# Half-size tiles for the score levels, and a new order at the stage edges, in a two-layer HGRN2/GLA encoder step

## The chip, the cores and the metric

The kernel runs on one core of a Trainium2 chip. The metric is the device time of one execution in microseconds (us). Engines are named as in the profile: PE is the matrix engine's matmuls, PEld its weight loads (they overlap the matmuls), DVE the vector engine, ACT the scalar engine, POOL the GpSimd engine, SP the engine whose queue issues the DMAs.

## The reference

Two groups of tokens go through the same two layers: 1024 tokens of one prompt, and 8 streams of 16 tokens each. Together they are 1152 tokens, nine tiles of 128.

```
layer 0: m = hgrn2_mixer(x)   # 8 heads, key width 128, value width 128
layer 1: m = gla_mixer(x)     # 4 heads, key width 128, value width 256
x = layer_norm(ALPHA * x + m);  x = layer_norm(ALPHA * x + conv_ffn(x))   # in both layers

# both mixers, per head, logf the log of a data-dependent forget gate:
b      = cumsum(logf)
scores = einsum('td,sd,tsd->ts', q, k, exp(b[t] - b[s]))      # s <= t
o      = scores @ v + (q * exp(b)) @ S
S_new  = exp(b_last) * S + (k * exp(b_last - b)).T @ v
```

The feed-forward part is `gelu(causal_conv3(a)) * b @ w_down` with `[a|b] = x @ w_up` and 2816 columns.

## The kernel before

**Matmuls.** Each weight and each activation is split into a rounded part (`_hi`) and a remainder (`_lo`), and a product is three matmuls (`mm3`, L770 to L772). Products that aren't split are plain float32 matmuls; the trace shows two PE instructions for each of those (x16 for eight tiles).

**Scores by levels.** Within a tile of 128 tokens the scores are found in seven levels, `LEVELS = [64, 32, 16, 8, 4, 2, 1]`. At level m a query in the second half of a block of 2m tokens meets the keys in the first half of that block, both decayed to the block's middle. For level x the DVE subtracts (`sub`, L1579), ACT takes the exponentials, the DVE multiplies by k and q (`decay`, L1595 and L1596), PE multiplies per token tile (L1021), and the DVE copies what the level's mask allows from PSUM to the score tile `a` (`place_scores`, L1608). A matmul of level x loads `128 - m` keys (at least 68) as weights and streams 64 queries. The first three levels of prompt tiles have 8 tiles (the streams' blocks begin at m = 8), the others 9. The last level is a matmul of 128 keys by 192 columns per tile (L1005), whose diagonal and pair scores are copied by L1621 and L1629. The prompt's scores go to banks 0 and 1 by turns, those of the last level to banks 1 to 5.

**A head.** PE's order in a head is written out: the projection of the next head's keys or queries, the transposes of the decayed keys (L891), the streams' part (L899, eight matmuls by turns on four groups of 32 output partitions), states (L912, L933), the second projection, outputs (L965, L967), and then the list `MERGED`: level 0, value/gate tiles 0 and 1, then level x followed by value/gate tile x + 1. A value/gate tile is 24 matmuls. In the h layer, `rest_early` (L1647) makes the remainders of the next head's weights on the DVE, in levels 4 and 5 of the list.

**Waits that the change touches.** `scores_taken` makes the next head's first projection wait until all scores are out of PSUM, since it writes banks 0 to 2. The last transposes of a layer wait for the same and for the last value tile. At the edge between the layers POOL splits the first GLA head's value and gate weights, and their DMAs wait until the rank-16 projection (`r_pe`) is done. `AFTER` lists which transposes follow which sum of the output projection; a normalized tile `("n", t)` must be ready on the DVE (L1519) before it is transposed. `last_outputs` is the DVE's order at the end of a layer's mixer, `gate` (L1804, L1806) within it.

## Time and profile before

| | |
|---|---|
| median of 3 runs | 2972.05 us (2970.08 to 2974.06) |
| the profiled execution's own time | 2972.53 us |
| its span, first to last instruction | 2970.7 us |
| granted clock, mean | 0.993 |
| PE busy | 2915.5 us, 98% |
| DVE, ACT, POOL busy | 1654.6, 711.7, 913.0 us |

PE is busy nearly all the time, so the table of busy shares alone says little; what matters is how long each PE instruction holds the engine, and the few places where PE stands idle. The granted clock is TensorE's, as a share of 2.4 GHz.

### The profile page before, as it was taken

Reading aid. Unit: us, or ns where it says so; the run is one execution under the profiler, and the core shown is the slowest. Engines: PE = TensorE matmul, PEld = TensorE weight load, DVE = VectorE, ACT = ScalarE, POOL = GpSimd, SP = SyncE. Lnnn points to the kernel's source line nnn. Section 1 sums busy time; section 2 is a strip of 40 time slices with the busy share of each in tenths; the row PEclk is TensorE's granted clock in tenths of the full one; section 3 lists DMA queues with packets and bytes.
Section 4 is the critical chain, followed back from the end, with each engine's and each line's share of the span. In section 5 each row is a group of like instructions: output and inputs, shape, how many; then the busy total and the mean of one; then the engine's idle time right before and its main releaser. Section 6 shows DMA issues by size and latency. Waiting matters only on the chain.

```text
span 2970.7 us, 41990 instructions
## 1 busy us (share of the span) xinstructions
PE 2915.5 (98%) x16893; PEld 2706.4 (91%) x16893; DVE 1654.6 (56%) x2229; ACT 711.7 (24%) x1332; POOL 913.0 (31%) x396
## 2 busy tenths in 40 slices
PE   8999999999999999999998999999999999999998
PEld 8999999978999999999987888887899999999997
DVE  5777777776544444444465456557654444444446
ACT  4444444431111111111123334332111111111112
POOL 2111111131533333333236214213153333333324
PEclk9999999999999999999999999999999999999999
DMA  4111111131111111111022112204111111111102
GB/s 127 44 44 43 43 43 43 57 111 36 57 43 43 42 42 42 42 42 42 29 77 92 40 35 72 65 22 123 39 57 43 43 42 41 42 41 41 42 30 92
DMA packets 189918, 155.82 MB, mean 52 GB/s; under 512 B 7144, under 2 KB 173120, under 8 KB 189760
## 3 DMA queue, kind: packets, MB, share of 16 engines
q1 hardware_dynamic: 189836, 154.64, 16.8%
q8 instruction: 61, 1.00, 0.1%
q14 instruction: 21, 0.17, 0.0%
HBM read 135.34 MB, written 19.28 MB: 52 GB/s over the span
## 4 chain that ended last, share of the span: by engine, by line
PE 91%; DVE 4%; ACT 2%; issue 1%; POOL 1%; DMA 0%; POOLq 0%; SPq 0%; ACTq 0%; DVEq 0%
PE psum L770 27%; PE psum L772 27%; PE psum L771 27%; PE psum L1021 4%; PE psum L1005 1%; PE psum L804 1%; PE psum L912 1%; DVE stats L1505 1%; ACT h_junk L1197 0%; PE psum L965 0%; PE psum L891 0%; POOL ring_lo L703 0%; PE psum L967 0%; DVE tm L1955 0%; PE psum L933 0%
## 5 line engine op out<-in xcount | busy, mean ns | idle before, releaser
L700 POOL TENSOR_TENSOR ring_hi<-ring_raw,ones 128x1024 fp32r<-128x1024 f32 x181 | 388.8, 2148 | 1930.5 <-DMA ring_raw<-in_ffn_w_up 724.1
L770 PE MATMUL psum<-xt_hi,ring_hi 128*128 128x384 f32 (+1 forms) x2712 | 914.0, 337 | 13.3 <-DVE h_a L1629 4.3
L771 PE MATMUL psum<-xt_lo,ring_hi 128*128 128x384 f32 (+1 forms) x2712 | 911.5, 336 | 0.0
L772 PE MATMUL psum<-xt_hi,ring_lo 128*128 128x384 f32 (+1 forms) x2712 | 911.3, 336 | 0.0
L770 PEld LDWEIGHTS psum<-xt_hi,ring_hi 128*128 128x128 f32 (+1 forms) x2712 | 510.2, 188 | 25.8 <-issue 6.6
L771 PEld LDWEIGHTS psum<-xt_lo,ring_hi 128*128 128x128 f32 (+1 forms) x2712 | 510.3, 188 | 3.0 <-issue 0.4
L772 PEld LDWEIGHTS psum<-xt_hi,ring_lo 128*128 128x128 f32 (+1 forms) x2712 | 510.3, 188 | 2.2 <-issue 0.5
L703 POOL TENSOR_TENSOR ring_lo<-ring_raw,ring_hi 128x1024 fp32r<-128x1024 f32 x181 | 461.7, 2551 | 14.2
L770 PE MATMUL psum<-ring_hi,xt_hi 128*128 128x256 f32 (+1 forms) x1152 | 399.7, 347 | 4.9 <-POOL ring_lo L703 4.9
L772 PE MATMUL psum<-ring_hi,xt_lo 128*128 128x256 f32 (+1 forms) x1152 | 388.9, 338 | 0.0
L771 PE MATMUL psum<-ring_lo,xt_hi 128*128 128x256 f32 (+1 forms) x1152 | 388.4, 337 | 0.0
L1919 DVE TENSOR_TENSOR tm<-tm,psum 128x512 f32<-128x512 f32 x360 | 247.5, 688 | 242.4 <-PE psum L772 237.2
L770 PE MATMUL psum<-ring_hi,h_hi 128*128 128x512 f32 x792 | 309.1, 390 | 0.0
L772 PE MATMUL psum<-ring_hi,h_lo 128*128 128x512 f32 x792 | 308.8, 390 | 0.0
L771 PE MATMUL psum<-ring_lo,h_hi 128*128 128x512 f32 x792 | 308.7, 390 | 0.0
L1888 DVE TENSOR_SCALAR cv<-ax,params 128x1024 f32<-128x1024 f32 x88 | 52.8, 643 | 435.2 <-ACT ax L1197 435.2
L1197 ACT ACTIVATE ax<-psum 128x384 f32<-128x384 f32 (+2 forms) x176 | 67.5, 411 | 853.5 <-PE psum L772 853.5
L770 PEld LDWEIGHTS psum<-ring_hi,xt_hi 128*128 128x128 f32 x1152 | 219.4, 190 | 26.6 <-POOL ring_lo L703 5.3
L772 PEld LDWEIGHTS psum<-ring_hi,xt_lo 128*128 128x128 f32 x1152 | 219.0, 190 | 23.4
L771 PEld LDWEIGHTS psum<-ring_lo,xt_hi 128*128 128x128 f32 x1152 | 219.5, 191 | 21.0
L1890 DVE SCALAR_TENSOR_TENSOR cv<-ax,params,cv 128x1024 f32<-128x1024 f32 (+1 forms) x176 | 213.1, 1252 | 10.4 <-DVE cv L1888 3.2
L772 PEld LDWEIGHTS psum<-ring_hi,h_lo 128*128 128x128 f32 x792 | 148.7, 188 | 30.9
(198 smaller groups left out, 2978.2 us busy)
## 6 DMA issues: line engine op xcount, KB each, us to landing
ring_raw<-in_ffn_w_up SPq DMA_DIRECT2D x88, 512.0 KB, 3.8
ring_raw<-in_ffn_w_down SPq DMA_DIRECT2D x44, 512.0 KB, 3.9
tm<-in_x_prompt SPq DMA_DIRECT2D x16, 512.0 KB, 6.7
ring_raw<-in_hgrn_w_in SPq DMA_DIRECT2D x16, 512.0 KB, 5.3
ring_raw<-in_hgrn_w_in SPq DMA_DIRECT2D x32, 256.0 KB, 3.7
ring_raw<-in_gla_w_in SPq DMA_DIRECT2D x32, 256.0 KB, 4.1
x_scratch<-tm SPq DMA_DIRECT2D x9, 512.0 KB, 2.6
tm<-x_scratch SPq DMA_DIRECT2D x9, 512.0 KB, 6.9
```

Of the source, the lines that this page charges most:

```text
L700: nc.gpsimd.tensor_tensor(ring_hi[slot][:, 0:width], ring_raw[slot][:, 0:width], ones[:, :].to_broadcast([P, width]), ALU.mult).then_inc(u ...
L703: nc.gpsimd.tensor_tensor(ring_lo[slot][:, 0:width], ring_raw[slot][:, 0:width], ring_hi[slot][:, 0:width].bitcast(F32), ALU.subtract).the ...
L770: nc.tensor.matmul(dst, w_hi, x_hi, start=start, stop=False)
L771: nc.tensor.matmul(dst, w_hi, x_lo, start=False, stop=False)
L772: return nc.tensor.matmul(dst, w_lo, x_hi, start=False, stop=stop)
L804: last = nc.tensor.transpose(w_bank(layer, job)[:, k * P:(k + 1) * P], tm[:, t, kk * P:(kk + 1) * P], ident[:, :])
L912: last = nc.tensor.matmul(bank[b][:, x * dv:(x + 1) * dv], tile["kt"][:, c, :], tile["v"][:, c, :], start=True, stop=True)
L1021: last = nc.tensor.matmul(scores(x, t).rearrange("p (g w) -> p g w", w=m), ct[:, 0:level_keys(x)], queries, start=True, stop=True)
L1197: return nc.scalar.activation(*a, **k)
L1888: ins = V.tensor_scalar(dst, tap(0), param(f, 0), param(f, 3), ALU.mult, ALU.add)
L1890: ins = V.scalar_tensor_tensor(dst, tap(j), param(f, j), dst, ALU.mult, ALU.add)
L1919: V.tensor_tensor(x, x, bank[6 + n][:, :], ALU.add).then_inc(AD.sem, 1)
```

## The change

All levels under 64 tokens, and the last one, are made in two halves of a token tile: 64 keys as weights, half of the queries (32, or 96 columns in the last level) streamed, and the result written to output partitions 0 to 63 or 64 to 127. A block of at most 64 tokens lies wholly in one half, so the scores that are left out are those that the mask threw away. Matmul instructions double, columns per instruction halve. The DVE copies by halves too. The last level's scores go to banks 3 to 5.

Beside this: `rest_early` moves behind `place_scores(NL - 2)`; the next head's first projection no longer waits for the last level's copies; a layer's last transposes use banks 0 to 2 and wait neither for the copies nor for the last value tile; the GLA gate's low-rank matmuls of chunks 1 and 2 move behind the streams' states; the DMAs of three of the first GLA head's four value/gate units are issued ahead of the last two stores of x2, and POOL splits them in the order 0, 2, 3, 1; the last two token tiles of layer 1's input are transposed within the projection of chunk 1; tile n0 is transposed after sum 5 and n1 after sum 6 of the output projection; the feed-forward's first b chunk goes ahead of the last a chunk; the last DVE work of a mixer is reordered; POOL's third output unit waits for `gated`; in the very first head ACT takes the key exponential ahead of a value tile. A remainder is the `_lo` part of a split.

```diff
-AFTER[4], AFTER[5] = [("n", 0)], [("n", 1)]
+AFTER[5], AFTER[6] = [("n", 0)], [("n", 1)]
 for _t in range(EARLY, NT):
     if _t + 2 < NT:
-        AFTER[2 * _t] = [("o", _t + 2)]
+        AFTER[2 * _t] = AFTER[2 * _t] + [("o", _t + 2)]
...
+        def key_banks(last_):
+            return ((0, 0, 4), (1, 4, 8), (2, 8, 9)) if last_ else ((6, 0, 4), (3, 4, 8), (4, 8, 9))
...
+        def in_halves(x):
+            return LEVELS[x] < HALF
+        def half_scores(x, t, hf):
+            c = 0 if t == PT else t * (HALF // 2)
+            return level_bank(x, t == PT)[hf * HALF:(hf + 1) * HALF, c:c + HALF // 2]
...
-        def pair_scores(t):
-            c = t % 2 * 2 * P
-            return bank[1 + t // 2][:, c:c + 3 * HALF]
+        def pair_scores(t, hf):
+            return psum[hf * HALF:(hf + 1) * HALF, 3 + t // 4, t % 4 * P:t % 4 * P + 3 * HALF // 2]
...
+                    for u in GLA_FIRST_UNITS[:-1]:
+                        vg_unit(KIND["g"], 0, u)
                 sp.wait_ge(ln_done, NT + t + 1)
                 sp.dma_start(x2_dram[t * P:(t + 1) * P, :], tm[:, t, :]).then_inc(res_io[t], 16)
+            sp.wait_ge(SIG["g"]["r_pe"].sem, 3)
+            vg_unit(KIND["g"], 0, GLA_FIRST_UNITS[-1])
...
+                    if u == 2:
+                        pool.wait_ge(S["gated"].sem, S["gated"].at(heads, 0))
...
+            for x, u in enumerate(GLA_FIRST_UNITS):
+                split(U_G + 2 + x, 2 + u, slot_count("g", 0, 2 + u), skipped=4)
...
-                        wait("pred", i - 1, preds_after(LAST - 1) if c == 0 else S["pred"].per)
+                        wait("pred", i - 1, preds_after(LAST - 1))
...
-                    wait("vg", p, NT)
-                    if last_:
-                        wait("pred", p, S["pred"].per)
-                    for jb, (b, tiles) in enumerate(((6, range(0, 4)), (3, range(4, 8)), (4, range(8, 9)))):
-                        for x, t in enumerate(tiles):
+                    for jb, (b, t0, t1) in enumerate(key_banks(last_)):
+                        if b == 3:
+                            wait("pred", p, S["pred"].per)
+                        if b == 6:
+                            wait("vg", p, NT)
+                        for x, t in enumerate(range(t0, t1)):
                             last = nc.tensor.transpose(bank[b][:, x * P:(x + 1) * P], tile["c0"][:, t * P:(t + 1) * P], ident[:, :])
                         last.then_inc(S["kt_pe"].sem, 1)
+                    wait("vg", p, NT)
...
+                def low_rank(chunks):
                     pe.wait_ge(S["wgk_in"].sem, S["wgk_in"].at(i, 16))
                     pe.wait_ge(S["rt"].sem, 3)
-                    for c in range(NC):
+                    for c in chunks:
...
+                if n == "g" and not last_:
+                    low_rank(range(0, 1))
...
+                    low_rank(range(1, NC))
...
-                                last = nc.tensor.matmul(pair_scores(t), tile["k"][:, t * P:(t + 1) * P],
-                                                        tile["q3"][:, t * HALF:(t + 1) * HALF, :].rearrange("p g w -> p (g w)"),
-                                                        start=True, stop=True)
+                                for hf in range(2):
+                                    q0 = t * HALF + hf * (HALF // 2)
+                                    last = nc.tensor.matmul(pair_scores(t, hf), tile["k"][:, 2 * q0:2 * q0 + HALF],
+                                                            tile["q3"][:, q0:q0 + HALF // 2, :].rearrange("p g w -> p (g w)"),
+                                                            start=True, stop=True)
...
+                                if in_halves(x):
+                                    for hf in range(2):
+                                        ch = c[:, t * P + hf * HALF:t * P + (hf + 1) * HALF]
+                                        queries = ch.rearrange("p (g w) -> p g w", w=2 * m)[:, :, m:2 * m]
+                                        last = nc.tensor.matmul(half_scores(x, t, hf).rearrange("p (g w) -> p g w", w=m), ch, queries,
+                                                                start=True, stop=True)
+                                    continue
...
+                    weights_split(0)
+                    pe.wait_ge(F["a_out"].sem, F["a_out"].at(0, 0))
+                    for c in range(NC - 1):
+                        pe.wait_ge(tj_lo, w_job(layer, "n", TPC * (c + 1) - 1, 1) + 1)
+                        chunk(0, c)
+                    pe.wait_ge(ln_done, (2 * layer + 1) * NT)
+                    for hf in range(2):
+                        transpose_half(layer, "n", NT - 1, hf)
+                    weights_split(1)
+                    pe.wait_ge(params_rd, layer + 1)
+                    pe.wait_ge(F["mult"].sem, F["mult"].at(0, 0))
+                    chunk(1, 0)
+                    pe.wait_ge(tj_lo, w_job(layer, "n", NT - 1, 1) + 1)
+                    chunk(0, NC - 1)
+                    for c in range(1, NC):
+                        chunk(1, c)
...
+                            if c == 1 and (done, k) in (("q_proj", 0), ("q_proj", 6)):
+                                next_operand(NT - 2 if k == 0 else NT - 1)
...
+                if not ahead:
+                    take_vg(NL - 1)
                 wait("kh_sub", i, 2)
                 activate(tile["c0"][:, :], tile["c0"][:, :], ACT.Exp, scale=-K["scale"]).then_inc(S["kh_exp"].sem, 1)
+                if ahead:
+                    take_vg(NL - 1 + ahead)
...
+                            if in_halves(x):
+                                w = HALF // 2
+                                for hf in range(2):
+                                    h = slice(hf * HALF, (hf + 1) * HALF)
+                                    dst = tile["a"][h, t0:t1, h].rearrange("p t (g w) -> p t g w", w=2 * m)[:, :, :, m:2 * m]
+                                    src = level_bank(x, t0 == PT)[h, 0:nt * w].rearrange("p (t g w) -> p t g w", t=nt, w=m)
+                                    msk = level_mask[h, x * HALF + hf * w:x * HALF + (hf + 1) * w].rearrange("p (g w) -> p g w", w=m)
+                                    last = V.copy_predicated(dst, msk.unsqueeze(1).to_broadcast([HALF, nt, w // m, m]), src)
+                                last.then_inc(S["pred"].sem, 1)
+                                continue
...
-                    if n == "h" and x in (4, 5):
-                        rest_early(x - 4)
...
+                if n == "h":
+                    rest_early(0)
+                    rest_early(1)
...
                 chain_states(K, p, True)
+                gate(K, p)
                 new_streams(K, p, True, range(STREAMS_FIRST[n]))
-                for t in range(1, EARLY):
-                    rest_half(layer, "o", t, 0)
-                gate(K, p)
...
-                    take_o(K, p, True, (0, 1))
+                    take_o(K, p, True, (0,))
+                    rest_half(layer, "o", 1, 0)
+                    take_o(K, p, True, (1,))
                     apply_gate_early()
                     take_o(K, p, True, (2,))
                     apply_rms_early()
+                    rest_half(layer, "o", 2, 0)
                     take_o(K, p, True, (3,))
```

On PE, in the first h head, this is the end of the level list; `h_c` is the decayed key/query tile, `ring` the value/gate weights. Before, PE's rows read:

```order
L771 MATMUL psum<-ring_lo_79,xt_hi 128x256
L772 MATMUL psum<-ring_hi_78,xt_lo 128x256
L1021 MATMUL psum<-h_c_106 126x64 x9
L1005 MATMUL psum<-h_q_113,h_k 128x192 x9
L770 MATMUL psum<-ring_hi_75,xt_hi 128x256
L771 MATMUL psum<-ring_lo_76,xt_hi 128x256
L772 MATMUL psum<-ring_hi_75,xt_lo 128x256
```

In the change, PE's rows at the same place read:

```order
L801 MATMUL psum<-ring_lo_79,xt_hi 128x256
L802 MATMUL psum<-ring_hi_78,xt_lo 128x256
L1062 MATMUL psum<-h_c_106 64x32 x18
L1044 MATMUL psum<-h_q_113,h_k 64x96 x18
L800 MATMUL psum<-ring_hi_75,xt_hi 128x256
L801 MATMUL psum<-ring_lo_76,xt_hi 128x256
L802 MATMUL psum<-ring_hi_75,xt_lo 128x256
```

Both levels have twice the matmuls, with 64 weight columns and half of the streamed ones; nothing else has moved between the value/gate matmuls.

On the DVE, in the same head, from the subtraction of level 3 on; `h_a` is the score tile, `h_b` the running sum of log gates, and `ring_lo` the remainders. Before, the DVE's rows read:

```order
L1579 TENSOR_TENSOR h_c_105<-h_b 128x1152
L1608 COPY_PREDICATED h_a<-level_mask,psum 112x32x16
L1647 TENSOR_TENSOR ring_lo_70<-ring_raw_71,ring_hi_69 128x1024
L1595 TENSOR_TENSOR h_c_105<-h_c_105,h_k 128x144x4
L1596 TENSOR_TENSOR h_c_105<-h_c_105,h_q 128x144x4
L1579 TENSOR_TENSOR h_c_106<-h_b 128x1152
L1608 COPY_PREDICATED h_a<-level_mask,psum 120x64x8
L1608 COPY_PREDICATED h_a<-level_mask,psum 120x8x8
L1647 TENSOR_TENSOR ring_lo_73<-ring_raw_74,ring_hi_72 128x1024
L1595 TENSOR_TENSOR h_c_106<-h_c_106,h_k 128x288x2
L1596 TENSOR_TENSOR h_c_106<-h_c_106,h_q 128x288x2
```

In the change, the DVE's rows read so, from the last level's copy of level 4's scores on:

```order
L1677 COPY_PREDICATED h_a<-level_mask,psum 64x8x8x4 x2
L1677 COPY_PREDICATED h_a<-level_mask,psum 64x8x4 x2
L1657 TENSOR_TENSOR h_q_113<-h_q_113,h_q 128x576
L1735 TENSOR_TENSOR h_c_105<-h_b 128x128
L1738 TENSOR_TENSOR h_c_105<-h_b 128x1024
L1743 COPY h_dec<-h_e 128x8
L1744 COPY h_dec<-h_e 128x8
L1677 COPY_PREDICATED h_a<-level_mask,psum 64x8x16x2 x2
L1677 COPY_PREDICATED h_a<-level_mask,psum 64x16x2 x2
L1724 TENSOR_TENSOR ring_lo_70<-ring_raw_71,ring_hi_69 128x1024
L1724 TENSOR_TENSOR ring_lo_73<-ring_raw_74,ring_hi_72 128x1024
L1755 TENSOR_TENSOR h_c_105<-h_c_105,h_k 128x1152
```

The two `ring_lo` rows stood between the levels' copies and multiplications; they now stand behind the copies of level 5 and ahead of the multiplication (128x1152) that the key transposes wait for.

On SP's queue, at the edge between the layers (`x_scratch` is the stored x2, `ring_raw_77`, `80`, `83` and `86` are the four slots of value/gate units). Before, SP's rows read:

```order
L670 DMA x_scratch<-tm 128x1024 x7
L667 DMA ring_raw_74<-in_gla_w_in 128x8x128
L670 DMA x_scratch<-tm 128x1024 x2
L517 DMA ring_raw_77<-in_gla_w_in 128x2x256 x2
L517 DMA ring_raw_80<-in_gla_w_in 128x2x256 x2
L517 DMA ring_raw_83<-in_gla_w_in 128x2x256 x2
L517 DMA ring_raw_86<-in_gla_w_in 128x2x256 x2
L526 DMA g_s_142<-in_state_gla 128x8x256
```

In the change, SP's rows there read:

```order
L694 DMA x_scratch<-tm 128x1024 x7
L689 DMA ring_raw_74<-in_gla_w_in 128x8x128
L549 DMA ring_raw_77<-in_gla_w_in 128x2x256 x2
L549 DMA ring_raw_83<-in_gla_w_in 128x2x256 x2
L549 DMA ring_raw_86<-in_gla_w_in 128x2x256 x2
L694 DMA x_scratch<-tm 128x1024 x2
L549 DMA ring_raw_80<-in_gla_w_in 128x2x256 x2
L539 DMA g_s_142<-in_state_gla 128x8x256
```

Three of the four units are now issued ahead of the last two stores; the fourth, whose slot holds the rank-16 weights, stays behind them.

## Rows read from the trace of the kernel before

**Rows 1.** The page, busy time of each engine

```profile
PE 2915.5 (98%) x16893; PEld 2706.4 (91%) x16893; DVE 1654.6 (56%) x2229; ACT 711.7 (24%) x1332; POOL 913.0 (31%) x396
```

**Rows 2.** Waits of PE: total us, times, longest

```profile
PE psum L804 <- DVE tm L1519: 5.2, 3, 2.8
PE psum L770 <- POOL ring_lo L703: 4.9, 1, 4.9
PE psum L770 <- DVE h_a L1629: 4.3, 1, 4.3
...
PE psum L770 <- DVE g_s L1737: 3.2, 3, 1.1
PE psum L770 <- DVE xt_lo L1499: 3.1, 2, 1.6
PE psum L804 <- DVE tm L1768: 2.4, 1, 2.4
...
PE psum L891 <- DVE h_a L1629: 0.9, 1, 0.9
PE psum L891 <- issue: 0.8, 1, 0.8
```

**Rows 3.** Timeline of PE, levels 1, 5 and 6 of h head 2

```profile
205.71 1.57 PE L1021 MATMUL psum<-h_c 128*96 128x64 f32 x16 [0.42 <-DVE h_c L1596]
207.09 0.36 PE L770 MATMUL psum<-ring_hi,xt_hi 128*128 128x256 f32 x1
...
224.09 2.09 PE L1021 MATMUL psum<-h_c 128*126 128x64 f32 x18
225.98 0.37 PE L770 MATMUL psum<-ring_hi,xt_hi 128*128 128x256 f32 x1
...
228.93 3.09 PE L1005 MATMUL psum<-h_q,h_k 128*128 128x192 f32 x18
231.73 0.42 PE L770 MATMUL psum<-ring_hi,xt_hi 128*128 128x256 f32 x1
```

**Rows 4.** Groups of PE by form, level 0

```profile
L1021 PE MATMUL psum<-h_c 128*68 128x64 f32 x128 | 9.2, 225 | 1.1 <-DVE h_c L1596 1.1
```

**Rows 5.** Timeline of PE, the streams' part of h head 1

```profile
178.71 0.65 PE L899 MATMUL psum<-h_s,h_qz 128*32 128x128 f32 x16
179.35 0.38 PE L912 MATMUL psum<-h_v,h_kt 128*128 128x128 f32 x1
```

**Rows 6.** Window of 0.05 us, L899 alone: us, PE busy (in flight), PEld busy (in flight)

```profile
178.70:178.75 0.05, 0.04 (x4) 0.05 (x7) 1.00 0.00 0
```

**Rows 7.** Timeline of PE: first of 24 matmuls with 16, then 128 weight columns

```profile
1571.36 0.34 PE L770 MATMUL psum<-xt_hi,ring_hi 128*16 128x384 f32 x1
...
1575.52 0.34 PE L770 MATMUL psum<-xt_hi,ring_hi 128*128 128x384 f32 x1
```

**Rows 8.** Timeline of the DVE, levels 2 to 4 of h head 2

```profile
209.22 1.35 DVE L1579 TENSOR_TENSOR h_c<-h_b 128x1152 f32<-128x1152 f32 x1
...
211.90 0.76 DVE L1595 TENSOR_TENSOR h_c<-h_c,h_k 128x576 f32<-128x576 f32 x1 [0.68 <-ACT h_c L1197]
...
213.24 1.35 DVE L1579 TENSOR_TENSOR h_c<-h_b 128x1152 f32<-128x1152 f32 x1
...
215.11 1.22 DVE L1647 TENSOR_TENSOR ring_lo<-ring_raw,ring_hi 128x1024 fp32r<-128x1024 f32 x1
```

**Rows 9.** Window at head 1's first projection: PE, PEld, DVE, ACT, POOL busy, clock

```profile
92.00:99.00 7.00, 4.92 (x15) 4.92 (x16) 6.96 (x7) 0.00 (x0) 6.92 (x3) 0.51 0.01 2
```

**Rows 10.** Timeline of POOL at the edge between the layers

```profile
1593.97 1.89 POOL L700 TENSOR_TENSOR ring_hi<-ring_raw,ones 128x1024 fp32r<-128x1024 f32 x1 [8.89 <-DMA ring_raw<-in_gla_w_in]
```

**Rows 11.** Timeline of PE, two waits of layer 1 and what follows the first

```profile
1615.53 0.80 PE L770 MATMUL psum<-ring_hi,xt_hi 128*128 128x512 f32 x1 [4.95 <-POOL ring_lo L703]
...
1629.28 2.50 PE L1021 MATMUL psum<-g_c 128*68 128x64 f32 x32
...
2013.60 1.01 PE L965 MATMUL psum<-g_v,g_a 128*128 128x256 f32 x2 [1.99 <-DVE g_v L1793]
```

108 lines of the change are left out of this document (56 added, 52 removed).

## The prediction

> **What bounds the kernel now.** I read the page's busy times first: PE is busy 2915.5 us, and its weight loads 2706.4 [rows 1]. So the time is what PE's instructions take one after another, plus a few waits. The waits of PE came next. Those of over 1 us are few, and each has one cause [rows 2]. Then I read the timeline of a steady h head. There the distance from one row's start to the next group's start is what the group costs, since matmuls overlap: level 1 costs 207.09 - 205.71 = 1.38 us for 16 instructions, level 5 costs 1.89 for 18, the last level 2.80 for 18 [rows 3]. Levels 2, 3 and 4 read the same way: 1.50, 1.81 and 1.86. The six levels that change cost 11.24 us in a head, and twelve heads have them: 135 us.
>
> What holds such an instruction? Level 5 streams 64 columns and takes 1.89 / 18 = 105 ns. Level 0 streams 64 too, but loads 68 weight columns instead of 126, and takes (9.2 / 8 - 0.225) / 15 = 62 ns [rows 4]. So levels 1 to 5 are bound by the load of weights, at some 0.83 ns a column (105 / 126). The last level, 192 columns in 2.80 / 18 = 156 ns [rows 3], is bound by streaming, 0.81 ns a column.
>
> **The halves.** The change makes 32 or 36 instructions of 64 weight columns out of 16 or 18 wide ones. If the two halves of a tile ran one after the other, an instruction would take 64 x 0.83 + 3 = 57 ns, and a level would cost 1.8 to 2.05 us, more than before. All depends on whether two halves that write different partitions run side by side. The streams' part is the nearest row: 16 instructions of 32 weight columns and 128 streamed ones start within 0.65 us [rows 5], 40 ns each, where one such stream alone takes 128 x 0.81 = 104 ns. In its first 0.05 us four matmuls and seven loads are in flight [rows 6], where one after another the seven loads alone would take 7 x 32 x 0.83 = 186 ns: groups do run side by side, in loads and in streams.
>
> The Trainium skill says the same in "TensorEngine Tiling (Array Packing)", Key Properties, but adds a rule against this change: a switch of the tiling mode drains the engine. By that rule, at the bound worked out next, the time would be 2901 instead of the 2884 below.
>
> What a drain could cost is bounded by rows. Between the last of 24 matmuls with 16 weight columns and the first with 128 I see nothing: 1575.52 - 1571.36 = 4.16 us for 24, 173 ns each, which is what the 128-wide ones take too [rows 7]. Behind the streams' part the next matmul starts only when all have ended [rows 5], 0.65 us from the first, where four passes of 0.104 make 0.42; the rest, 0.23 us, is the most that a drain can have cost there, and part of it is a wait for ACT's copy. With 6 exits in 12 heads the bounds are 0 and 17 us. I take 0, as the first row has no other wait in it.
>
> So I take a pair of halves at 56 ns, loads side by side: a tile's two passes take 0.112, levels 1 and 2 cost 0.90 us each, levels 3 to 5 cost 1.01 each, and the last, with 96 columns x 0.81 + 4 = 82 ns per pair, 1.48. Together 6.3 instead of 11.24: **4.9 us a head**.
>
> Is PE still the bound then? In GLA heads a value/gate tile takes 5.4 us and covers the DVE: 4 x 4.9 = **19.6**. In h heads PE's step would be 0.9 to 1.0 plus 24 x 0.12 = 2.88, so 3.8 to 3.9 us, and the DVE's is 213.24 - 209.22 = 4.02 us: subtract, wait for ACT, multiply [rows 8]. The copies of halves (some 0.3 us more per level) fit between the subtraction's end at 210.57 and the multiplication at 211.90 [rows 8], of which 0.68 was idle. The two remainders of 1.22 us [rows 8] would have made two of these steps 4.4; they now lie behind the levels, where the DVE waits for PE's last level anyhow. Before, PE's steps of 4.5 to 4.8 us let the DVE gain on it at every level, and the new steps nearly match; I take 4.6 per head, seven heads, **32.2**. In the first head the last level follows level 5 directly, and the DVE needs 2.9 us between them (PE 1.0), then its copies for the ninth tile: **2.4**.
>
> **The waits, one by one.** (1) Head 1's first projection waited 4.3 us for the pair copies [rows 2] and then ran at half clock: of the 7 us from 92 the clock is 0.51, PE busy 4.92 [rows 9], so about 2.4 us lost. Banks 3 to 5 make the wait needless: **6.7**. The key exponential is taken early, so the transposes 12.5 us later find their keys. (2) The edge between the layers. POOL began the four units at 1593.97, after 8.89 us idle for a DMA [rows 10], and PE waited 4.95 us for the last one, after which 48 matmuls took 13.7 us [rows 11]; at full clock they take 48 x 0.227 = 10.9. With three units' DMAs issued when the last down matmul is done, at 1571.4 [rows 7], POOL starts them when its own work ends, at 1593.97 - 8.89 = 1585.1, and four units that took 21.5 us are done by 1603 to 1607. The last two tiles' transposes, within a projection, save some 1.5 us of waiting and most of a slow projection after them. PE then reaches the value/gate tiles at about 1606 instead of 1615.5 and runs them at full clock: 9.5 + 2.8, less some for the DVE's level 1, which POOL slows: **12.0** (9 to 13.5). (3) Low-rank chunks 1 and 2 take 1.2 us and fill the wait of 1.06 for `g_s`: **3.2** [rows 2]. Their ACT work starts 1.2 us later, with tens of us before level 0. (4) The b chunk of 4.1 us covers the wait of 1.57 for tile 8's remainder, twice: **3.1** [rows 2]. Its conv comes 2.6 us later, and a whole a projection (12.5) lies between that and the next use of the banks. (5) Transposing n0 and n1 a sum (5.4 us) later removes 5.2 us of waits for L1519 [rows 2]. But n1 and o5 are now four half transposes in a row on two banks; the third waits for ACT and the DVE, about 1.2 us in each layer: **2.8**. (6) At the h layer's end the 2.4 us wait for L1768 and 0.9 for the copies go [rows 2]; the two remainders now delay the key product by 0.6 us, and `gate` comes ahead of a remainder that a sum needs: net **2.4** (0 to 3.3). (7) At the GLA layer's end the wait of 1.99 goes, since bank 7 is emptied earlier; behind it a pair of instructions took 1.01 [rows 11] where 0.6 is usual, and four steps at half clock lost about 1.7: **3.7**. The last transposes no longer wait 0.8 for the last value tile [rows 2]. POOL's third output unit waits for `gated` but ends 1 us ahead of its sum; if not, 1 to 3 us return.
>
> The waits sum to 6.7 + 12.0 + 3.2 + 3.1 + 2.8 + 2.4 + 3.7 + 0.8 = 34.7, the levels to 19.6 + 32.2 + 2.4 = 54.2. From the profiled execution's 2972.5 (span 2970.7 and 1.8 around it; the median of the runs is 0.5 less) this leaves 2883.6; I forecast **2884 us**.
>
> **Rivals.** (A) *Halves run side by side, but something else paces them.* Level 0's 62 ns [rows 4] is more than 68 x 0.83 + 3 = 59. If it is a floor for issuing any PE instruction, a level's 32 to 36 need 2.0 to 2.2 us of issue; with 24 slower matmuls between, only level 1 of each h head, which PE meets with an empty queue, pays about 1.1: 2893. If the DVE's step comes out at 4.3 instead of 4.02, five steps pay 1.4 a head, 2894; both, 2903. 20 in 100.
>
> The Trainium skill names such a floor in "TensorE: Matmul & The Clock Gate", about 62 ns per matmul on the sequencer in one decoding mode; level 0's row agrees with it, though a load of 68 columns explains nearly as much.
>
> (B) *Halves run one after another at 57 ns.* Levels would cost 1.8, 1.8, 2.05 (three times) and 2.95, so 12.7 against 11.24: 12 x 1.5 = 18 lost, 34.7 won, 2956. [Rows 6] speaks against it. 8 in 100. (C) *One after another at the floor of 62*: 13.6 a head, 28 lost, 2966. 4 in 100. (D) **Slower:** *each change from one half to the other drains the array.* An instruction then waits out the other's 0.225 us [rows 4] instead of following after 62 ns, 0.16 a change. A head has 98 changes: 12 x 0.16 x 98 = 188 us on top of (C), and the time is about 3154. It decides from little: (C) is only 6.5 us below before, so 5 ns per change make it slower. What is in flight in [rows 6] speaks against it. 6 in 100.
>
> **Chances and range.** The forecast has 62 in 100. Its own range is 2868 (h heads keep all of 4.9 to 5.2, the edge gives 13.5) to 2901 (exits of 0.23). The range for 8 in 10 takes in (A) and some of its sum with the exits: 2867 to 2915. It leaves out B, C, D. Within 0.2% (6 us, about what a measurement here can tell from no change) lies half of C. Faster: 62 + 20 + 8 + 2 = 92, same 2, slower 6.
>
> **What the profile would show.** Levels 1 to 5 with rows of 32 and 36 instructions that take 0.9 to 1.1 us from start to next start, and loads of two halves in flight at once; an h head of 68.1 us instead of 72.7, a GLA head of 98 instead of 104. No wait at head 1's projection and clock 1.0 there; value/gate tiles of the first GLA head near their predecessor's end; `n1` and `o5` with a wait of about 1 us. The forecast is wrong if these levels cost 1.8 us or more (B to D), or if PE waits at each level for the DVE's product (A).

## The result, and the profile after

The changed kernel takes 2921.3 us (median of 4 runs, 2920.0 to 2925.5), against 2973.1 for the kernel before, measured beside it: a ratio of 0.9831, 95% interval 0.9817 to 0.9844. It is faster by 51.8 us where 88.9 were forecast, and 6 us above the range's upper end. The profiled execution is the slowest of the four, 2925.5 us, 47.1 less than before's 2972.5; what follows accounts for those 47.

The page of the changed kernel, busy time of each engine (before: [rows 1]):

```profile
PE 2871.5 (98%) x18141; PEld 2645.2 (90%) x18141; DVE 1678.0 (57%) x2349; ACT 712.1 (24%) x1332; POOL 907.1 (31%) x396
```

PE has 1248 more instructions and is busy 44 us less. Its waits in the changed kernel (before: [rows 2]):

```profile
PE psum L834 <- DVE xt_lo L1564: 8.3, 3, 5.4
...
PE psum L1044 <- DVE h_a L1677: 5.7, 2, 3.8
PE psum L1062 <- DVE g_c L1661: 3.4, 1, 3.4
...
PE psum L834 <- DVE tm L1846: 2.4, 1, 2.4
...
PE psum L927 <- issue: 2.0, 1, 2.0
PE psum L800 <- issue: 1.8, 3, 0.7
```

The waits of [rows 2] are gone but for the 2.4 us of the tail (then L1768, now L1846). Five others stand in their place, and none was in the forecast at that size. The half levels, in the timeline of PE of a steady h head (before: [rows 3]):

```profile
199.94 0.28 PE L802 MATMUL psum<-ring_hi,xt_lo 128*128 128x256 f32 x1
200.15 1.12 PE L1062 MATMUL psum<-h_c 128*64 128x32 f32 x32
201.20 0.39 PE L800 MATMUL psum<-ring_hi,xt_hi 128*128 128x256 f32 x1
201.42 0.28 PE L801 MATMUL psum<-ring_lo,xt_hi 128*128 128x256 f32 x1
201.54 0.28 PE L802 MATMUL psum<-ring_hi,xt_lo 128*128 128x256 f32 x1
...
204.27 1.24 PE L1062 MATMUL psum<-h_c 128*64 128x32 f32 x36
205.44 0.39 PE L800 MATMUL psum<-ring_hi,xt_hi 128*128 128x256 f32 x1
...
216.99 2.00 PE L1044 MATMUL psum<-h_q,h_k 128*64 128x96 f32 x36
218.91 0.39 PE L800 MATMUL psum<-ring_hi,xt_hi 128*128 128x256 f32 x1
```

From 32 instructions to 36 a level grows by 1.17 - 1.05 = 0.12 us, about the 0.112 forecast for a tile. But 8 tiles take 1.05 and not 0.90. And the first half starts 0.21 us behind the value/gate matmul ahead of it, where a wide level started 0.12 us behind its own, in the timeline of PE before:

```profile
223.97 0.28 PE L772 MATMUL psum<-ring_hi,xt_lo 128*128 128x256 f32 x1
224.09 2.09 PE L1021 MATMUL psum<-h_c 128*126 128x64 f32 x18
225.98 0.37 PE L770 MATMUL psum<-ring_hi,xt_hi 128*128 128x256 f32 x1
226.19 0.28 PE L771 MATMUL psum<-ring_lo,xt_hi 128*128 128x256 f32 x1
```

Behind the level the next step takes 0.21 us there and 0.22 in the changed kernel, so almost nothing is added on that side. Some 0.15 + 0.09 us is thus paid per level, not per tile. (The last level's 1.92 us holds a wait besides; see `e8` below.)

Read by stages, each the distance between two rows of PE's timeline, in us (levels and waits of the forecast put where they lie). The last stage ends where the feed-forward's last transposes begin (L1168, now L1232); what follows takes 63.7 us in both kernels:

| stage | before | after | gained | forecast |
|---|---|---|---|---|
| start to head 0's level 0 | 55.4 | 56.3 | -0.9 | 0 |
| head 0's level 0 to head 1's | 70.3 | 62.8 | 7.5 | 9.1 |
| six h heads | 6 x 72.67 | 6 x 69.55 | 18.8 | 27.6 |
| last h head's level 0 to the key transposes | 40.3 | 41.4 | -1.1 | 4.6 |
| h layer's end, output projection, feed-forward | 900.5 | 902.7 | -2.2 | 4.0 |
| edge, to the first GLA level 0 | 126.8 | 113.9 | 12.9 | 12.0 |
| first GLA head | 94.4 | 95.2 | -0.8 | 6.0 |
| two GLA heads | 210.4 | 200.1 | 10.3 | 11.9 |
| last GLA head's level 0 to the key transposes | 63.0 | 58.7 | 4.3 | 5.7 |
| layer 1's end, output projection, feed-forward | 909.9 | 911.5 | -1.6 | 8.0 |

Both the steady heads and the stages between them fell short. The first row is mostly chance: in it PE waits for the first tokens, and in the traces of this study it takes 53.7 to 57.1 us.

### The profile page after: what moved, and what is told of

Its sections match the earlier page's. It is cut to its first block, busy times and chain, and to the rows that moved or that the text cites. A ratio compares the mean times of both kernels' runs of the same rounds, so it can differ in the third digit from the quotient of the medians.

```text
span 2923.5 us, 44633 instructions
## 1 busy us (share of the span) xinstructions
PE 2871.5 (98%) x18141; PEld 2645.2 (90%) x18141; DVE 1678.0 (57%) x2349; ACT 712.1 (24%) x1332; POOL 907.1 (31%) x396
## 4 chain that ended last, share of the span: by engine, by line
PE 83%; DVE 9%; ACT 4%; issue 3%; DMA 0%; POOL 0%; ACTq 0%; POOLq 0%; DVEq 0%; SPq 0%
PE psum L800 26%; PE psum L802 26%; PE psum L801 26%; DVE h_c L1644 1%; ACT h_c L1259 1%; DVE h_c L1661 1%; PE psum L834 1%; PE psum L945 1%; PE psum L1062 1%; DVE h_a L1677 1%; ACT g_c L1259 1%; DVE stats L1570 1%; PE psum L968 0%; ACT h_junk L1259 0%; ACT L1259 0%
## 5 line engine op out<-in xcount | busy, mean ns | idle before, releaser
L729 POOL TENSOR_TENSOR ring_lo<-ring_raw,ring_hi 128x1024 fp32r<-128x1024 f32 x181 | 459.1, 2537 | 14.2
L1973 DVE SCALAR_TENSOR_TENSOR cv<-ax,params,cv 128x1024 f32<-128x1024 f32 (+1 forms) x176 | 202.9, 1194 | 10.4 <-DVE cv L1971 3.2
```

Of the source, the lines that this page charges most:

```text
L729: nc.gpsimd.tensor_tensor(ring_lo[slot][:, 0:width], ring_raw[slot][:, 0:width], ring_hi[slot][:, 0:width].bitcast(F32), ALU.subtract).the ...
L1973: ins = V.scalar_tensor_tensor(dst, tap(j), param(f, j), dst, ALU.mult, ALU.add)
```

## Experiments

Two theories. **S**: halves run side by side at the forecast's pace, but changing the array's tile size costs a fixed time per level, and the rest was lost in new waits, each with a cause of its own in the order of DVE and POOL work. **Rivals**: the pace itself is worse than forecast; or most of the gain came from the edges and not from the halves. Every median below is beside before's 2971 to 2972 on the same chip.

**The kernel again.** `e4_after_again` is the changed kernel, unedited.

> The changed kernel itself, for the spread of its own waits between executions. Both theories: 2919 to 2926. The waits behind DVE and POOL work (3.8 and 5.4 us) are there again if they come from the order of work, and vary by more than 1 us if they come from chance.

2923.6 us. The wait ahead of the last h head's ninth tile came back as 3.84 us (3.83 in the first profile), that of layer 1 as 5.23 instead of 5.41. They belong to the order of work.

**Halves alone.** `e1_halves_only` is the kernel before with half levels:

```diff
-                                last = nc.tensor.matmul(pair_scores(t), tile["k"][:, t * P:(t + 1) * P],
+                                for hf in range(2):
+                                    q0 = t * HALF + hf * (HALF // 2)
+                                    last = nc.tensor.matmul(pair_scores(t, hf), tile["k"][:, 2 * q0:2 * q0 + HALF],
```

> The kernel before, with levels 1 to 6 in halves (the last one's scores in banks 3 to 5) and nothing else of the change: every wait, every order, the transposes and the remainders stay as before. Theory S (the pairs run at the forecast's pace, but each of the six levels costs 0.26 us more for going in and out of the half tiles): 3.1 us less per h head and 3.5 per GLA head on PE, of which the remainders, still made within levels 4 and 5, take back 0.5 to 1 in h heads, so 2936 to 2942. The forecast's own pricing (4.9 us a head, in and out free): 2919 to 2926. If most of the measured gain came from the edges, not from the halves: 2955 or more.

2963.8 us, 0.9967 (0.9953 to 0.9981): only 8 us faster, so S's 2936 to 2942 was missed, and by its number the run falls to the rival that most of the gain came from the edges. The trace tells why it doesn't. Here are two waits of PE in a steady h head, and that of the last one:

```profile
152.54 1.24 PE L1035 MATMUL psum<-h_c 128*64 128x32 f32 x36 [0.92 <-DVE h_c L1615]
...
159.18 0.39 PE L1017 MATMUL psum<-h_q,h_k 128*64 128x96 f32 x4 [0.88 <-DVE h_a L1631]
...
594.34 0.58 PE L1017 MATMUL psum<-h_q,h_k 128*64 128x96 f32 x4 [7.74 <-DVE h_a L1631]
```

An h head lasts 71.38 us (before 72.67), a GLA head 3.34 less than before. In h heads PE now waits for the DVE, twice per head. `e16_halves_moved` adds one thing, the two remainders behind level 5's copies:

```diff
                 for x in range(2, NL):
                     sub(x)
                     place_scores(x - 2)
-                    if n == "h" and x in (4, 5):
-                        rest_early(x - 4)
                     decay(x)
...
                 place_scores(NL - 2)
+                if n == "h":
+                    rest_early(0)
+                    rest_early(1)
```

> The kernel of e1_halves_only (halves alone, 2964) with the two remainders moved behind level 5's copies and nothing else. If the missing gain of the halves in h heads was the DVE's step (0.9 us waits ahead of level 5 and of the ninth tile in each head, 7.7 in the last), an h head falls from 71.4 to 69.5 us and the last head's wait to about 4: 2964 - 6 x 1.9 - 4 - 2 = 2947. If the waits have another cause, 2964.

2943.8 us: 20 us for moving two DVE instructions. An h head falls to 69.50 us and the last head's wait from 7.74 to 3.84. So the halves are worth 28 us once the DVE keeps pace, and the other edits of the change together 2943.8 - 2921.3 = 22.5. That settles the rival: the edges gave less than half of the gain, and less than the 34.7 us forecast for them.

**The pace of halves.** `e2_wide_levels` makes levels 1 to 5 wide again in the changed kernel; `e3_halves_apart` keeps the halves but issues all first ones, then all second ones:

```diff
# e2_wide_levels
         def in_halves(x):
-            return LEVELS[x] < HALF
+            return False
# e3_halves_apart
-                            for t in range(PT + (1 if x >= DEC_FROM else 0)):
-                                if in_halves(x):
-                                    for hf in range(2):
+                            for hf in range(2 if in_halves(x) else 0):
+                                for t in range(tiles):
```

> The changed kernel with levels 1 to 5 as full-width matmuls again; the last level stays in halves and the whole order of edges stays changed. Theory S: levels 1 to 5 give back 8.44 - 6.1 = 2.3 us a head, 12 heads 28 us, so about 2949, a little less if the DVE uses the time to catch up. The forecast's pricing: 3.6 a head, 43 us, 2964. An h head then lasts 71.8 us (S).

> The changed kernel, but in levels 1 to 5 all tiles' first halves are issued, then all tiles' second halves: the same instructions, no neighbours on different partitions. If two halves gain by running side by side (S and the forecast), a level of 32 instructions goes from 1.06 to about 1.9 us and 60 levels cost 45 to 50 us: 2966 to 2971. If half-size loads are simply cheaper one after another, no change: 2921.

2944.5 and 2965.1 us. In `e2` an h head lasts 71.58 us and a later GLA head 102.26, so halves in levels 1 to 5 give 2.0 and 2.2 us a head, near S's 2.3. In the timeline of `e3` a level of 32 instructions reads:

```profile
199.41 1.84 PE L1062 MATMUL psum<-h_c 128*64 128x32 f32 x32 [0.43 <-DVE h_c L1661]
201.18 0.39 PE L800 MATMUL psum<-ring_hi,xt_hi 128*128 128x256 f32 x1
```

1.77 us instead of 1.05, for the same instructions in another order. The gain comes from neighbours that write different partitions; one after another a half takes 1.77 / 32 = 55 ns, near the 57 of (B). That it is under 62 also shows that PE has no floor of 62 ns here, which was the first half of rival (A). The Trainium skill's floor of about 62 ns per matmul in one decoding mode ("TensorE: Matmul & The Clock Gate", "Wait — 56ns, not 53.3ns?") isn't in force for these instructions.

**What a change of tile size costs.** One more wide matmul per level, once amid the halves and once behind them:

```diff
                                 if in_halves(x):
                                     for hf in range(2):
...
+                                    if t == 3:    # e5_wide_middle; e6_wide_end: the level's last tile
+                                        wt = c[:, 4 * P:5 * P]
+                                        last = nc.tensor.matmul(level_bank(x, False)[0:level_keys(x), 256:256 + HALF].rearrange("p (g w) -> p g w", w=m),
+                                                                wt[:, 0:level_keys(x)], wt.rearrange("p (g w) -> p g w", w=2 * m)[:, :, m:2 * m], start=True, stop=True)
```

> The changed kernel with one more full-width matmul in each of levels 1 to 5, in the middle of the halves (behind tile 3), into columns of the bank that nobody reads. It adds 2 instructions of some 105 ns and one more change out of the half tiles and back into them, 60 times. Theory S (the 0.26 us per level is the price of the change of tile size): 60 x (0.21 + 0.26) = 28 us over the changed kernel's 2922, so 2950, and 15 us above the same matmul at the level's end. If the 0.26 us is something else (the change of instruction line, the wait for the DVE's semaphore, the last column's way through the array): 60 x 0.21 = 13 us, 2935, the same as at the end.

> The same extra full-width matmul, but behind the last half of each of levels 1 to 5, where the next value/gate matmul has full width anyhow: no further change of tile size. Both theories: 60 x 0.21 = 13 us, 2935, some of it perhaps hidden where PE waited for the DVE (0.4 us in level 1 of each h head is ahead of it and stays).

2938.9 and 2927.8 us. Level 3 of an h head, first in the timeline of `e5_wide_middle`:

```profile
207.00 0.66 PE L1062 MATMUL psum<-h_c 128*64 128x32 f32 x16
207.59 0.42 PE L1066 MATMUL psum<-h_c 128*120 128x64 f32 x2
207.94 0.78 PE L1062 MATMUL psum<-h_c 128*64 128x32 f32 x20
208.64 0.39 PE L800 MATMUL psum<-ring_hi,xt_hi 128*128 128x256 f32 x1
```

and then in that of `e6_wide_end`:

```profile
207.76 1.24 PE L1062 MATMUL psum<-h_c 128*64 128x32 f32 x36
208.94 0.43 PE L1066 MATMUL psum<-h_c 128*124 128x64 f32 x2
209.17 0.36 PE L800 MATMUL psum<-ring_hi,xt_hi 128*128 128x256 f32 x1
```

The two wide instructions hold PE for 0.35 us between halves and for 0.23 ahead of wide ones. Over whole heads it is 71.57 against 70.22 us: 1.35 for five more changes there and back, **0.27 us each**. The whole kernels differ by 11 us and not by the 16 that 60 changes would make, since in `e6` the GLA heads' second projection ran partly at half clock (14.2 us instead of 12.6, mean granted clock 0.88; a head of 102.28 us, 100.04 in the changed kernel), which hides `e5`'s extra there. Both lie below S's absolute figures: with PE slower, it waits less for the DVE, in the last h head (39.3 us to the key transposes in `e6` instead of 41.4) and in the first GLA head (91.3 instead of 95.2, behind an edge that is 1.5 longer).

What the two runs show is the price of one more run of half tiles. That all of it belongs to the change of size is argued: in `e3` the step of 0.21 us into the level is the same, but 32 instructions at 55 ns leave no room for the other 0.15, so that part may be what it takes until two halves go side by side.

The Trainium skill states a cost of such a change without a number ("TensorEngine Tiling (Array Packing)", Key Properties: a change of tiling mode drains the engine); the runs fit it, at 0.27 us.

**n0 and n1.** `e7_n_early` puts them back; `e12_n_spread` never puts more than two half transposes behind one sum:

```diff
# e7_n_early
-AFTER[5], AFTER[6] = [("n", 0)], [("n", 1)]
+AFTER[4], AFTER[5] = [("n", 0)], [("n", 1)]
# e12_n_spread
-AFTER[5], AFTER[6] = [("n", 0)], [("n", 1)]
...
-    AFTER[2 * _t + 1] = [("n", _t - 1)]
+for _t, _x in enumerate((5, 7, 9, 11, 13, 14, 15, 17)):
+    AFTER[_x] = [("n", _t)]
```

> The changed kernel with n0 after sum 4 and n1 after sum 5 again, as before the change. The trace of the changed kernel says that n1 and o5 together cost 1.6 us in layer 0, and in layer 1 a wait of 5.4 and some 1.9 us at half clock behind it, since the DVE norms a whole token tile ahead of the remainder that frees the bank; before, these waits were 1.2 and 2.75 + 1.24. So undoing this part gains about 0.3 + 3.3 = 3.6 us: 2918. The forecast's pricing (moving them later gains 2.8) would give 2925.

> The changed kernel, but no sum of the output projection has more than two half transposes behind it: n0 after sum 5, n1 to n3 after 7, 9 and 11, n4 to n6 after 13 to 15, n7 after 17, o5 alone after sum 6. If the loss is four half transposes in a row whose banks wait for remainders behind a whole norm on the DVE, 1.6 us go in layer 0, and 5.3 with 1.9 at half clock in layer 1: 2912 to 2914. If it is the DVE's backlog itself that PE meets there, whatever it transposes: 2919 to 2921.

2918.4 and 2915.2 us. This is the wait in the changed kernel, PE's timeline first:

```profile
2013.84 1.97 PE L834 MATMUL psum<-ident,tm 128*128 128x128 f32 x8 [5.41 <-DVE xt_lo L1564]
```

and the DVE's, up to the remainder that PE waits for:

```profile
2007.95 1.28 DVE L1570 BATCH_NORM_STATS2 stats<-tm 128x6 f32<-128x512 f32 x2
...
2009.92 1.27 DVE L1580 SCALAR_TENSOR_TENSOR tm<-tm,moments,ln_att 128x1024 f32<-128x1024 f32 x1
2011.30 1.29 DVE L1584 SCALAR_TENSOR_TENSOR tm<-tm,inv_std,ln_att 128x1024 f32<-128x1024 f32 x1
2012.50 0.68 DVE L1922 SCALAR_TENSOR_TENSOR tm<-tm,psum 128x512 f32<-128x512 f32 x1
2013.09 1.28 DVE L1564 TENSOR_TENSOR xt_lo<-psum,xt_hi 128x512 fp32r<-128x512 f32 x2
```

PE had the first two halves done at 2008.4. Their remainder is queued on the DVE behind the norm of a whole token tile. In `e12` both waits are gone and layer 1's end and feed-forward take 904.7 us instead of 911.5. Behind head 0's first level `e7`'s profile is 7.4 us shorter than that of `e4`, the changed kernel run again; 4.5 of them lie at the edge and in the first GLA head, by the clock (below), and n0 and n1 account for 3.

**POOL and the last h head.** The DVE's timeline in the last h head of the changed kernel:

```profile
562.64 1.95 DVE L1735 TENSOR_TENSOR h_c<-h_b 128x128 f32<-128x128 f32 x1
564.51 1.21 DVE L1738 TENSOR_TENSOR h_c<-h_b 128x1024 f32<-128x1024 f32 x1
565.65 2.31 DVE L1743 COPY h_dec<-h_e 128x8 f32<-128x8 f32 x1
...
568.06 1.95 DVE L1677 COPY_PREDICATED h_a<-level_mask,psum 64x256 f32<-64x256 uint8 x4
570.05 4.41 DVE L1724 TENSOR_TENSOR ring_lo<-ring_raw,ring_hi 128x1024 fp32r<-128x1024 f32 x2
```

POOL's timeline beside it:

```profile
561.79 2.65 POOL L726 TENSOR_TENSOR ring_hi<-ring_raw,ones 128x1024 fp32r<-128x1024 f32 x1 [43.97 <-PE psum L1062]
564.52 3.41 POOL L729 TENSOR_TENSOR ring_lo<-ring_raw,ring_hi 128x1024 fp32r<-128x1024 f32 x1
```

In a steady head without POOL the DVE's same instructions take 0.28 (L1735), 0.17 (L1743) and 2.36 us (the two of L1724). Three edits:

```diff
# e8_free_ninth: level 5's ninth tile in another bank
-            return bank[4 + x % 2 if sample else 1 - x % 2]
+            return bank[2 if x == NL - 2 else 4 + x % 2] if sample else bank[1 - x % 2]
...
-                                if t == PT:
-                                    wait("pred", i, preds_after(x - 1))
# e9_pool_free
-                    if u == 2:
-                        pool.wait_ge(S["gated"].sem, S["gated"].at(heads, 0))
# e10_pool_early: their DMAs go ahead of the last head's projection
-                pool.wait_ge(S["lvl_pe"].sem, S["lvl_pe"].at(heads - 1, NL - 1))
                 for u, slot in enumerate(W_SLOTS[layer]):
+                    if u == 2 * (1 - layer):
+                        pool.wait_ge(S["lvl_pe"].sem, S["lvl_pe"].at(heads - 1, NL - 1))
```

> The changed kernel with level 5's ninth tile in bank 2 instead of bank 5, so that the last level's ninth tile needn't wait for the DVE's copy. Theory S: 0.3 us in each of six h heads and 1.9 in the first go, 3.7 in all, so 2918; in the last h head the wait of 3.8 us only moves on to the key transposes and the streams' outputs, since there the DVE's own chain, slowed by POOL, ends at 580.5 whatever PE does. Rival: PE's waits are worth what they last, in the last h head too (3.8 and 1.4 of half clock behind it): 2913.

> The changed kernel, but POOL's third output unit no longer waits for the gate's product. If that wait only keeps POOL out of the DVE's way at no cost (the forecast), taking it away costs 0 to 2 us: 2921 to 2924. If it moved POOL's work onto the DVE's product that the tail waits for (L1846 took 1.97 us instead of 0.56 before, and the transposes still waited 2.4 us), that wait falls to about 1 and the 1.3 us in the GLA tail go, but the DVE's chain in the last h head, already slowed by POOL's first two units, ends up to 2 us later: 2919 to 2922. So no large change by either; what counts is which waits of the trace move.

> The changed kernel, but in the h layer the DMAs of the first two output units are issued ahead of the last head's projection and POOL splits them as soon as they are in, some 40 us earlier, instead of behind level 5 of the last head. If the last head's waits (3.8 ahead of the ninth tile with 1.4 at half clock behind it, 2.0 at the streams' outputs) come from POOL slowing the DVE there, they go: 7 us, less up to 2 where POOL now works, 2914 to 2916. If they come from the order of the DVE's work (the remainders behind level 5's copies), they stay: 2921.

2919.2, 2919.9 and 2920.2 us. `e8` shows what S said: a steady head is 0.26 us shorter (the last level takes 1.64 us instead of 1.92), head 0 loses its 1.9 us wait, and in the last head the wait moves on (3.5 us ahead of the key transposes, 3.85 ahead of L927). Taking away a wait on PE gained nothing where the DVE was the one that was late. In `e10` the last head's stretch falls from 41.4 to 36.7 us; POOL's work costs 1.8 us where it now lies. That its median gained only 1 to 3 us and missed the 2914 to 2916 expected, where the last head alone gained 4.7, is within what single executions of these kernels vary by. In `e9` L1846 takes 0.56 us again instead of 1.97, and the tail's wait falls from 2.4 to 0.6 us.

**The first GLA head.** In the changed kernel PE waits there, in its timeline and in the windows around (us, PE, PEld, DVE, ACT, POOL busy, granted clock, DMA):

```profile
1598.86 1.92 PE L1062 MATMUL psum<-g_c 128*64 128x32 f32 x32 [3.36 <-DVE g_c L1661]
```

```profile
1593.00:1598.00 5.00, 2.50 (x23) 2.08 (x21) 3.78 (x3) 1.70 (x4) 4.92 (x2) 0.99 0.00 0
1598.00:1603.00 5.00, 4.14 (x37) 3.61 (x38) 4.42 (x6) 1.70 (x4) 0.25 (x1) 0.50 0.01 3
```

POOL is busy up to 1598.3 and the DVE's product for level 1 takes 2.82 us; behind the wait the granted clock is 0.50 (1.2 of 2.4 GHz), and the level with its value/gate tile takes 9.4 us instead of 6.7. `e11_tile_first` puts each tile ahead of its level:

```diff
+                    for lv in range(1, NL):
+                        gla_order += [("vg", lv + 1), ("level", lv)]
```

> The changed kernel, but in the first GLA head each value/gate tile from the third on comes ahead of a level instead of behind it. The trace of the changed kernel shows PE waiting 3.4 us for the DVE's product of level 1, and 2.6 us more at half clock in what follows. A tile of 5.7 us covers the wait: 2916. If the DVE is simply behind by that much all the way, the wait moves on to level 2: 2921.

2921.7 us, no gain. But `e11`'s profile isn't comparable: in it, as in `e2` and `e5` to `e7`, a projection in front of this place took 14.2 us instead of 12.6 though PE waited for nothing there. In the windows of `e7` (the clock is 1.00 in the 3 us before and behind them):

```profile
1567.00:1570.00 3.00, 3.00 (x13) 2.32 (x12) 1.75 (x3) 2.90 (x5) 3.00 (x2) 0.80 0.52 178
1570.00:1573.00 3.00, 3.00 (x13) 3.00 (x12) 0.00 (x0) 2.97 (x3) 2.92 (x2) 0.63 0.00 0
```

PE came 1.5 us later, and so did POOL's next unit, which then hardly met two of the DVE's instructions ahead of level 1. In the DVE's timeline of the changed kernel they read:

```profile
1588.03 2.38 DVE L1661 TENSOR_TENSOR g_c<-g_c,g_q 128x512 f32<-128x512 f32 x1
1590.34 3.42 DVE L1644 TENSOR_TENSOR g_c<-g_b 128x1024 f32<-128x1024 f32 x1
```

and in that of `e7`:

```profile
1585.05 0.68 DVE L1661 TENSOR_TENSOR g_c<-g_c,g_q 128x512 f32<-128x512 f32 x1
1585.65 1.22 DVE L1644 TENSOR_TENSOR g_c<-g_b 128x1024 f32<-128x1024 f32 x1
```

So the DVE was ready when PE came. The dip is there in some traces and not in others, and with what it moves it gains 4.6 us: 115.4 + 89.1 us with it, 113.9 + 95.2 without. The clean comparison is `e13_together` against `e15_level_first`.

**All together.** `e13_together` is the changed kernel with `e8`, `e10`, `e11`, `e12`, and POOL's third output unit waiting for `qz` instead of `gated`; `e15_level_first` is the same without `e11`'s order; `e14_padded` is `e13` with 20 transposes of the identity at PE's start.

> The changed kernel with five things together: n0 to n7 spread (2915 alone), the first two output units of the h layer split early (2920 alone), POOL's third output unit waiting for the copy of the streams' queries instead of the gate's product, level 5's ninth tile in bank 2 (2919 alone), and the first GLA head's tiles ahead of its levels. If each cause is its own, the gains add: 7 + 2 + 3 + 1 or 2 from 2922, so 2907 to 2909, and some 4 less where the first GLA head no longer waits. If the clock and the waits trade with each other, 2912 or more.

> The kernel of e13_together with the first GLA head in the changed kernel's order again (a level, then its tile). If PE's wait of 3.4 us for level 1 there and the half clock behind it are real costs that the other order covers, 4 to 6 us more than e13_together; if the order gained nothing, as e11_tile_first's median of 2922 says, the same.

> The kernel of e13_together with 20 transposes of the identity matrix at the start of PE's program, where PE waits for the first tokens, into a bank that is written again before anyone reads it. It moves all later PE instructions by 20 places and adds nothing else. If the three waits of 0.5 to 1.1 us that the feed-forward loop of layer 1 shows at its turn (named issue) come from where the loop's instructions lie, they change or go: up to 2.6 us less than e13_together, or waits in the other layer. If they come from what runs beside PE there, they stay.

2902.4, 2907.9 and 2904.4 us (one of `e15`'s five executions took 2900.7, the others 2906.8 to 2908.8). The causes add up: `e13` is 0.9762 of before (0.9749 to 0.9776), 19 us below the changed kernel. Both profiles have 113.9 us to the first GLA level 0, and then 89.4 against 95.1 us, so the order covers the wait. The pad left `e14` with three waits of 0.6 us in the loop of the next item.

**The loop of layer 1's feed-forward.** In the changed kernel PE waits there at each of three turns of the loop, which no step of the change touches; it waited at none before. In the timeline of PE:

```profile
2324.08 0.43 PE L800 MATMUL psum<-xt_hi,ring_hi 128*128 128x384 f32 x1 [0.48 <-issue]
2473.99 0.43 PE L800 MATMUL psum<-xt_hi,ring_hi 128*128 128x384 f32 x1 [0.69 <-issue]
```

With what surrounds the waits a turn costs 0.8 to 1.0 us, 2.6 in all (up to 1.3 a turn in `e16`). `e17_shift_144` and `e18_shift_288` are `e13_together` with one and two waits (m = 1, 2), long satisfied, ahead of each group of matmuls of layer 1's output projection:

```diff
+                    for _ in range(m * layer):
+                        pe.wait_ge(ident_in, 16)
                     last = mm3(sum_bank(x)[:, :], xt_hi[:, k, t * P:(t + 1) * P], xt_lo[:, k, t * P:(t + 1) * P],
```

> The kernel of e13_together with one more wait (on the identity matrix's DMA, long done) ahead of each group of three matmuls of layer 1's output projection. Most of these waits fold into the matmul that follows, so the feed-forward loop of layer 1 moves by only about a dozen PE instructions. If the waits named issue at the loop's turn depend on where the loop lies, so small a shift leaves them: three of 0.5 to 1.1 us, 2902 to 2903.

> The same with two waits ahead of each group, of which one can't fold: the loop of layer 1 moves by about 140 PE instructions, and nothing else changes that PE waits for. If the place of the loop decides, the three waits go: 2.1 to 2.6 us less than e17_shift_144, so about 2900, and no row named issue in layer 1's loop. If the waits come from what runs beside PE there (they were absent before the change, present in layer 1 in most kernels since, in layer 0 in e2_wide_levels), they stay. The Trainium skill says in Runtime: NRT & Kernel Launch, Instruction fetch mechanics, that a taken branch to a place outside the fetched window stalls the engine; by that rule the place decides.

2902.0 and 2898.9 us. The pages' first lines, `e13_together`, `e17` and `e18`:

```profile
span 2901.9 us, 44622 instructions
```

```profile
span 2900.8 us, 44636 instructions
```

```profile
span 2898.5 us, 44766 instructions
```

14 more instructions in the trace leave the waits, 144 more remove all three, and layer 1's end and feed-forward fall from 903.9 to 900.9 us. The loop's place in the program decides; that fits `e2`, `e5` and `e6` too, where it also lies elsewhere and layer 1's loop shows no such wait (in `e2` that of layer 0 has three instead, 0.5 to 0.95 us). The Trainium skill has a rule for it (a taken branch out of the fetched window stalls; "Runtime: NRT & Kernel Launch", Instruction fetch mechanics), and the runs fit it, though no view names what PE waited for.

## Why the prediction was right in direction and short by 37 us

**Halves side by side: right.** The forecast's 0.112 us per tile is met (0.12 by the rows of 32 and 36 instructions), and `e3` shows the mechanism. A GLA head became 3.34 us shorter by the halves (`e1`); with 6 x 0.27 added that makes 4.96, where 4.9 was forecast. B, C and D are out.

**"With 6 exits in 12 heads the bounds are 0 and 17 us. I take 0": this step failed.** The cost is 0.27 us per change there and back (`e5` against `e6`), 72 x 0.27 = 19.4 us, half of what was missing and just past the upper bound. The rows add up to the same: the six levels take 2 x 1.05 + 3 x 1.17 + 1.64 = 7.25 us instead of the 6.3 forecast, and each is entered 0.09 and left 0.01 to 0.02 later, 1.6 us a head together. The bound came from the right row [rows 5]; the choice of 0 came from [rows 7], whose narrow matmuls have 16 weight columns but evidently aren't tiled as the halves are (argued, not tested). The Trainium skill's rule, set beside it at the bound of 0.23, gave 2901.

**The DVE's step in h heads: right, for the right reason.** PE showed no wait at levels 2 to 5 (at level 1 0.4 to 0.5 us, as before), and the moved remainders were worth 20 us (`e16`). The ninth tile's wait of 0.26 us per head was not foreseen (`e8`).

**The waits**, by the forecast's numbers:

- (1) Right. Head 1's projection: 6.7 forecast; from the last value/gate tile to head 1's level 0 it is 40.2 against 33.4 us, 6.8.
- (2) The edge: 12.9 to level 0, so right. But the term counted the DVE's level 1 as a small deduction, and it gave back 3.4 us of waiting and 2.7 at half clock (`e13` against `e15`).
- (3) The waits for `g_s` went, but a GLA head is only 0.45 us shorter for it (100.48 in `e1` to 100.04).
- (4) Right: both waits of 1.57 us are gone.
- (5) Wrong in sign. Priced as one wait for ACT and the DVE, 1.2 us, it was a wait behind a whole norm in the DVE's queue (1.6 and 5.4 us, and half clock behind the second); `e12` gives back 6 to 8.
- (6) Forecast +2.4, came as -2.9, since the tail kept its wait and PE lost 2.1 us at L927 and 1.6 at half clock behind the tail's wait. POOL's third unit, put off by `gated`, slowed L1846 to 1.97 us (`e9`). The DVE's chain in the last h head, slowed by POOL's first units, which stretch the two remainders to 4.41 us too, held PE 3.8 us at the ninth tile and 2.0 at L927; `e10` removes the first and 0.6 of the second.
- (7) Right (25.4 to 21.6 us), with a new 1.3 us wait beside it.

**The sum.** Missing against the forecast: 19.4 for the changes of tile size, 5.3 in the last h head, 5.3 at the h layer's end, 6.5 for n0 and n1, 6.0 in the first GLA head, 2.6 in the loop, 1.8 in (3), 1.3 in (7), 2.5 at the start (0.9, chance) and in head 0 (the ninth tile's wait of 1.9 us): 50.7. Against them stand 4.2 us of slow clock in two GLA heads' projections (14.1 and 15.3 us before, 12.6 now), which nobody had counted, and some 1 us each at the edge and in the h heads' levels. That leaves 44 to 45, where the gap is 41.8; the 3 us too many I can't place.

## What to carry to other kernels

Small tiles that write different partitions ran side by side here only where they were neighbours in program order, and each run of them costs a fixed time; so gather them into few long runs, and count entries before columns. When PE gets faster, read again who is queued on the DVE ahead of every instruction that frees a bank, and which POOL work lies beside it: removing PE's wait without its cause only moves it. And what moving two DVE instructions was worth beside the halves, 20 us (`e1` against `e16`), shows that an edit which looks like an accessory can be the one that lets the main one pay.

## What was not expected of the hardware

- A short DVE instruction suffers most beside POOL: a copy of 128x8 took 2.31 us instead of 0.17, a subtraction of 128x128 1.95 instead of 0.28, two of 128x1024 4.41 instead of 2.36.
- Going from wide tiles into half tiles and back costs 0.27 us: some 0.15 in the level itself (1.05 instead of the 0.90 that the pace gives), 0.09 ahead of it (its first half starts 0.21 us behind the wide matmul instead of 0.12), and next to nothing behind it (0.22 instead of 0.21).
- A loop's turn can cost PE 0.8 to 1.3 us or nothing, by the loop's place in the program; dead waits ahead of it, 144 more instructions in the trace, made the fastest kernel of this study, 2898.9 us, 0.9751 of before (0.9735 to 0.9768).
- PE's granted clock fell to half (0.50 from 1569.5 to 1571.5 us in `e7`) within a projection of 72 matmuls without any wait in it, in some traces and not in others with the same instructions there. The projection then took 14.2 us (mean clock 0.88) or 15.3 (0.78) instead of 12.6. A few us ahead of it PE runs matmuls with 16 weight columns (at the edge) or 16 rows (in later heads), at full clock, with the dip and without it. Why is open.
